# Turning the last gated block inside a down product: a change of order in the expert stage of a decoder step

## The chip, the cores and the metric

The kernel runs on one core of a Trainium2 chip. The metric is the device time of one execution in microseconds; three runs give a median. The profile is of one further execution, with its own time.

The engines have these names in the profile: PE is TensorE (PEld its weight loads), DVE is VectorE, ACT is ScalarE, POOL is GpSimd, SP is SyncE, which only issues transfers here.

## The reference, cut to what matters

One inference step of a two-layer decoder for 256 prompt tokens and 8 sample tokens, width 1024. The part that the change touches is the last one, a top-2-of-8 mixture of SwiGLU experts, each 1024 -> 3584 -> 1024:

```python
def swiglu(h, w1, w3, w2):
    return (jax.nn.silu(h @ w1) * (h @ w3)) @ w2

def moe_swiglu(h, w_router, b_router, w1, w3, w2):
    ...
    for e in range(N_EXPERTS):
        y = swiglu(h, w1[e], w3[e], w2[e]).astype(jnp.float32)
        out = out + dense_gate[..., e:e + 1] * y
```

All inputs are float32, and all eight experts' weights (3 x 1024 x 3584 each) are read once.

## The kernel before

**What came earlier.** Layer 0, the shared keys and values, attention and routing fill the first 775 us or so. Routing scatters the tokens' rows into a table of 128 slots for each expert, and the expert stage takes one expert after the other from it. For experts 0 to 6 the stage is a hardware loop; expert 7 is written out once more behind it.

**A product in three passes.** Every float32 operand is split into a high part (`_hi`, a rounded copy) and a low part (`_lo`, the remainder). A product is hi x hi + hi x lo + lo x hi, three matmuls of 128 x 128 by 128 x 512 each, made by the helper `three` (lines 477 to 479, so most matmuls carry one of these line numbers).

**Slabs.** An expert's weights come in 42 slabs of 1 MB (128 partitions x 2048 float32). The list `eslabs` gives their order. The hidden width is cut into seven blocks `j` of 512. For each block there are two slabs of w1, two of w3, and then the two slabs of w2 for the block before:

```python
for j in range(FCH):
    eslabs += [(1, j, 0), (1, j, 1), (3, j, 0), (3, j, 1)] + ([(2, j - 1, 0), (2, j - 1, 1)] if j else [])
eslabs += [(2, FCH - 1, 0), (2, FCH - 1, 1)]
```

So an expert's last slabs are w3 of block 6, w2 of block 5, w2 of block 6.

**The path of one slab.** SP issues its transfer into one of seven ring slots (`ring`, line 450) as soon as the slab seven places earlier has been split. ACT writes its high part (`w_hi`, `high`, line 1219) into one of three pair buffers: it waits until PE has used the slab three places earlier (`pair_used`) and until the transfer has landed. DVE writes the low part (`w_lo`, `low`, line 1715) when ACT is done with the high one. PE then does the slab's 12 matmuls.

**One expert on PE.** For each block `j`: the w1 product into bank 3 and the w3 product into bank 4 (`product`, 24 matmuls each on the rows `xe_hi`, `xe_lo`); between the two, the gated block of `j - 1` is turned by four PE transposes into bank 5 (`turn`, line 910); after them, `down(j - 1)`, 24 matmuls of the turned block with the two w2 slabs, into banks 6 and 7. Behind the last block the loop has no next w1 product, so three things follow each other on PE: `turn(6)`, then `turn_rows` (line 884: eight transposes of the next expert's rows into banks 0 and 1), then `down(6)`.

**What ACT and DVE do beside the slabs.** Each runs its instructions strictly in the order in which they are written, in a loop over `eslabs` that handles slab `k + 3` at place `k`:
- ACT: `silu` of bank 3 (line 1242) at (1, j, 1); `turned_high`, the high part of bank 5 into `upT_hi` (line 1233), for block `j - 1` right behind it; for block 6 at (2, 5, 1), after that place's `high`; then `gathered_high`, the high part of the next expert's rows (line 1224).
- DVE: the gating product, bank 4 times `silu`, into `up` (line 1741; its tile is named `phase` in the profile) at (3, j, 1), after that place's `low`; `turned_low`, the remainder of bank 5 into `upT_lo` (line 1730), for block `j - 1` at (1, j, 1) and for block 6 at (2, 5, 1), in each case after that place's `low`; then `gathered_low` (line 1720).

PE's `turn` waits for the gating product (`up_ready`) and for the previous remainder (`upT_ready`), and `down(j)` waits for `upT_ready` of block `j`. `turned_high` waits for `up_turned` from PE. The first product of the next expert waits for `xe_ready` from `gathered_low`. POOL stores an expert's output rows and fetches the rows of the next one but one when `turn_rows` has taken the last (512 KB each).

Of the kernel before, what the change touches and what calls it, by code (L numbers as in the profile page):

```python
# [5 lines left out]
F32 = mybir.dt.float32  # L6
F32R = mybir.dt.float32r
I32 = mybir.dt.int32
ALU = mybir.AluOpType
ACT = mybir.ActivationFunctionType  # L10
X = mybir.AxisListType.X

P = 128
# [16 lines left out]
FCH = FE // 512  # L30
# [5 lines left out]
SLOTS = 128  # L36
# [58 lines left out]
def yoco_step(nc, w, o):  # L95
# [24 lines left out]
    with ExitStack() as ctx:  # L120
# [12 lines left out]
        def over(name, other, skip, shape, dt):  # L133

            return nc.alloc_sbuf_tensor_at(name, shape, dt, offset=placed[other] + 4 * skip)
# [5 lines left out]
        bank = [wide[i // 2][:, 512 * (i % 2):512 * (i % 2 + 1)] for i in range(8)]  # L141
# [23 lines left out]
        tT = sb("tT", [P, KC, NT])  # L165
# [98 lines left out]
        gsel = mflat[0:1 + NB, D:D + P]  # L264
        grow = at(10240, D)[0:1 + NB, :]

        upT_hi = over("upT_hi", "tT", 0, [P, 4, P], F32R)
        upT_lo = over("upT_lo", "tT", 512, [P, 4, P], F32R)
        up_s = at(10240, 512)
        up = at(10752, 512)  # L270
        lg = at(11264, 3, NE)
# [23 lines left out]
        pair_used = sem("pair_used")  # L295
# [4 lines left out]
        xe_hi_ready, xe_ready, upT_hi_ready, upT_ready = (sem(n) for n in ("xe_hi_ready", "xe_ready", "upT_hi_ready", "upT_ready"))  # L300
# [75 lines left out]
        def used_by(e, c, m, j, half=1):  # L376

            return e * PER_E + (NSPLIT + c * NE * PER_E + eslabs.index((m, j, half)) + 1)
# [92 lines left out]
        def _(pe):  # L471
# [3 lines left out]
            def three(out, a, b, start, stop):  # L475

                pe.matmul(out, a[0], b[0], start=start, stop=False, skip_group_check=True)  # L477
                pe.matmul(out, a[0], b[1], start=False, stop=False, skip_group_check=True)  # L478
                return pe.matmul(out, a[1], b[0], start=False, stop=stop, skip_group_check=True)  # L479
# [208 lines left out]
            for c in range(LIN):  # L688
                for m in range(2):
                    i = 2 * c + m  # L690
# [160 lines left out]
            for c in range(3):  # L851
                for k in range(c + 1):
                    n = rows[k]
# [34 lines left out]
            def expert(e, c, last):  # L888

                def weights(m, j, half, rows):  # L890
                    k = eslabs.index((m, j, half))
                    pe.wait_ge(lo_done, e * PER_E + (NSPLIT + c * NE * PER_E + k + 1))
                    return [t[:, (NSPLIT + k) % PAIRS, :].rearrange("p (k n) -> p k n", k=rows) for t in (w_hi, w_lo)]

                def count(per, k):
                    return e * per + (c * NE * per + k)

                def product(m, j, bk):
                    for half in range(2):
                        hi, lo = weights(m, j, half, 4)  # L900
                        for i in range(4):
                            k = 4 * half + i
                            mm = three(bank[bk][0:SLOTS, :], (xe_hi[:, k, :], xe_lo[:, k, :]), (hi[:, i, :], lo[:, i, :]), k == 0, k == KC - 1)
                        mm.then_inc(pair_used, 1)

                def turn(j):
                    pe.wait_ge(up_ready, count(FCH, j + 2))
                    pe.wait_ge(upT_ready, count(FCH, j + 1))
                    for i in range(4):
                        mm = pe.transpose(bank[5][:, SLOTS * i:SLOTS * (i + 1)], up[0:SLOTS, P * i:P * (i + 1)], ident[0:SLOTS, 0:SLOTS])  # L910
                    mm.then_inc(up_turned, 1)

                def down(j):
                    pe.wait_ge(upT_ready, count(FCH, j + 2))
                    if j == 0:
                        pe.wait_ge(y0_copied, count(1, 1))
                        pe.wait_ge(y1_copied, count(1, 1))
                    for half in range(2):
                        hi, lo = weights(2, j, half, 2)
                        for i in range(2):  # L920
                            for q in range(2):
                                cols = slice(512 * q, 512 * (q + 1))
                                mm = three(bank[6 + q][0:SLOTS, :], (upT_hi[:, 2 * half + i, :], upT_lo[:, 2 * half + i, :]),
                                           (hi[:, i, cols], lo[:, i, cols]), j == 0 and half == 0 and i == 0, j == FCH - 1 and half == 1 and i == 1)
                        mm.then_inc(pair_used, 1)

                pe.wait_ge(xe_ready, count(1, 1))
                for j in range(FCH):
                    pe.wait_ge(silu_done, count(FCH, j + 1))
                    product(1, j, 3)  # L930
                    if j >= 1:
                        turn(j - 1)
                    pe.wait_ge(up_ready, count(FCH, j + 1))
                    product(3, j, 4)
                    if j >= 1:
                        down(j - 1)
                turn(FCH - 1)
                if not last:
                    turn_rows(e, c, 1)
                down(FCH - 1)  # L940
# [14 lines left out]
        def _(act):  # L955
# [271 lines left out]
            def expert(e, c, last):  # L1227
                def count(per, k):
                    return e * per + (c * NE * per + k)

                def turned_high(j):
                    act.wait_ge(up_turned, count(FCH, j + 1))
                    act.activation(upT_hi[:, :, :], bank[5][:, :].rearrange("p (k n) -> p k n", k=4), ACT.Copy).then_inc(upT_hi_ready, 1)

                for k, (m, j, half) in enumerate(eslabs):

                    if k + PAIRS < PER_E or not last:
                        high(e, c, k + PAIRS)
                    if (m, half) == (1, 1):
                        act.wait_ge(pair_used, used_by(e, c, 1, j))  # L1240
                        act.wait_ge(up_ready, count(FCH, j + 1))
                        act.activation(up_s[0:SLOTS, :], bank[3][0:SLOTS, :], ACT.Silu).then_inc(silu_done, 1)
                        if j >= 1:
                            turned_high(j - 1)
                    if (m, j, half) == (2, FCH - 2, 1):
                        turned_high(FCH - 1)
                        if not last:
                            gathered_high(e, c, 1)
                act.wait_ge(pair_used, used_by(e, c, 2, FCH - 1))
                act.wait_ge(y_free, count(1, 1))  # L1250
                act.activation(ye[0:SLOTS, 0:512], bank[6][0:SLOTS, :], ACT.Copy).then_inc(y0_copied, 1)
# [24 lines left out]
        def _(dve):  # L1276
# [440 lines left out]
            def gathered_low(e, c, ahead):  # L1717
                dve.wait_ge(xe_hi_ready, e + (c * NE + ahead + 1))
                for q in range(2):
                    ins = dve.tensor_tensor(xe_lo[:, 4 * q:4 * q + 4, :], bank[q][:, :].rearrange("p (k n) -> p k n", k=4),  # L1720
                                            xe_hi[:, 4 * q:4 * q + 4, :].bitcast(F32), ALU.subtract)
                ins.then_inc(xe_ready, 1)

            def expert(e, c, last):
                def count(per, k):
                    return e * per + (c * NE * per + k)

                def turned_low(j):
                    dve.wait_ge(upT_hi_ready, count(FCH, j + 1))
                    dve.tensor_tensor(upT_lo[:, :, :], bank[5][:, :].rearrange("p (k n) -> p k n", k=4),  # L1730
                                      upT_hi[:, :, :].bitcast(F32), ALU.subtract).then_inc(upT_ready, 1)

                for k, (m, j, half) in enumerate(eslabs):
                    if k + PAIRS < PER_E or not last:
                        low(e, c, k + PAIRS)
                    if (m, half) == (1, 1) and j >= 1:
                        turned_low(j - 1)
                    if (m, half) == (3, 1):
                        dve.wait_ge(pair_used, used_by(e, c, 3, j))
                        dve.wait_ge(silu_done, count(FCH, j + 2))  # L1740
                        dve.tensor_tensor(up[0:SLOTS, :], bank[4][0:SLOTS, :], up_s[0:SLOTS, :], ALU.mult).then_inc(up_ready, 1)
                    if (m, j, half) == (2, FCH - 2, 1):
                        turned_low(FCH - 1)
                        if not last:
                            gathered_low(e, c, 1)
                dve.wait_ge(pair_used, used_by(e, c, 2, FCH - 1))
                dve.wait_ge(y_free, count(1, 1))
                dve.tensor_copy(ye[0:SLOTS, 512:1024], bank[7][0:SLOTS, :]).then_inc(y1_copied, 1)
# [195 lines left out]
```

## Time and profile before

| | |
|---|---|
| time of the three runs | 1827.14, 1830.06, 1832.4 us; median 1830.06 us |
| the profiled execution | 1819.31 us, of which its span (first to last instruction) 1817.4 us |
| PE busy | 1627.1 us, 90% of the span |
| DVE busy | 1251.6 us, 69% |
| ACT busy | 983.4 us, 54% |
| transfers | 513.45 MB, 283 GB/s over the span |
| transfers of expert slabs | 336 of 1024 KB |
| mean granted PE clock | 0.927 of full speed |

How to read it: the span has stages with different limits, so shares of the whole say little about one stage. What matters here is the stage of the experts, which runs from about 778 us to 1783 us; the rows below are from that stage. Busy PE time includes matmuls that run at the lower of the two clock levels, so a busy PE is not always a fast one.

### The profile page before, as it was taken

What the parts mean: (1) busy time and instruction counts of PE and PEld (TensorE: products, weight loads), DVE (VectorE), ACT (ScalarE), POOL (GpSimd) and SP (SyncE); (2) the same over time, 40 slices, a digit from 0 to 9 for tenths busy, and PEclk for the clock granted to TensorE, in tenths of its full rate; (3) what the DMA queues carried; (4) which work ended last, traced back from release to release, by engine and by line L of the source; (5) the groups of instructions that cost most, each with busy time, mean ns of one, the idle gap of its engine ahead of it and who ended that gap; (6) DMA issues with size and microseconds to landing.
All of it is one profiled execution on the core that took longest, in us unless ns stands there. A gap on an engine that the chain in (4) does not pass through costs nothing.

```text
span 1817.4 us, 22939 instructions
## 1 busy us (share of the span) xinstructions
PE 1627.1 (90%) x8712; PEld 1323.3 (73%) x8712; DVE 1251.6 (69%) x1092; ACT 983.4 (54%) x881; POOL 135.0 (7%) x130
## 2 busy tenths in 40 slices
PE   6869999799897669789999999999999999999991
PEld 3459999498784446578788788788787887887881
DVE  2464543668772442478788788788787887887884
ACT  1134432333332332367677677677676776776771
POOL 0000000026431311100000000000000000000001
PEclk9679999899998759789999999999999999999996
DMA  9965545945468025689999899899899998998972
GB/s 322 349 211 186 180 151 180 304 159 199 161 226 305 0 70 210 243 307 368 333 381 381 309 395 375 309 388 378 310 391 353 345 382 306 388 379 310 387 287 85
DMA packets 249295, 513.45 MB, mean 283 GB/s; under 512 B 9977, under 2 KB 69545, under 8 KB 249217
## 3 DMA queue, kind: packets, MB, share of 16 engines
q1 hardware_dynamic: 243691, 492.49, 75.4%
q0 software_dynamic: 4768, 17.37, 2.5%
q10 hardware_dynamic: 766, 2.65, 0.4%
q8 instruction: 45, 0.74, 0.2%
q14 instruction: 25, 0.20, 0.0%
HBM read 498.58 MB, written 14.35 MB: 282 GB/s over the span
## 4 chain that ended last, share of the span: by engine, by line
PE 76%; DVE 12%; ACT 3%; issue 3%; POOL 3%; DMA 2%; SPq 0%; POOLq 0%; DVEq 0%; ACTq 0%
PE wide L477 22%; PE wide L478 21%; PE wide L479 21%; POOL phase L1787 2%; ACT w_hi L1219 2%; DVE phase L1491 2%; PE wide L537 2%; DVE w_lo L1715 2%; PE wide L526 1%; PE wide L910 1%; POOL phase L1793 1%; DVE w_lo L393 1%; DMA ring<-in_cache_v 1%; PE wide L758 1%; DMA ring<-in_ada_mix_w 1%
## 5 line engine op out<-in xcount | busy, mean ns | idle before, releaser
L1715 DVE TENSOR_TENSOR w_lo<-ring,w_hi 128x2048 fp32r<-128x2048 f32 x336 | 768.3, 2290 | 162.1 <-ACT w_hi L1219 161.7
L1219 ACT ACTIVATE w_hi<-ring 128x2048 fp32r<-128x2048 f32 x336 | 643.5, 1920 | 267.8 <-PE wide L479 267.7
L477 PE MATMUL wide<-w_hi,xe_hi 128*128 128x512 f32 x896 | 355.7, 397 | 6.7 <-DVE xe_lo L1720 5.0
L479 PE MATMUL wide<-w_hi,xe_lo 128*128 128x512 f32 x896 | 350.2, 391 | 0.0
L478 PE MATMUL wide<-w_lo,xe_hi 128*128 128x512 f32 x896 | 349.8, 390 | 0.0
L477 PE MATMUL wide<-tHi,w_hi 128*128 128x264 f32 x672 | 198.4, 295 | 28.2 <-DVE mLo L1409 28.2
L478 PE MATMUL wide<-mLo,w_hi 128*128 128x264 f32 x736 | 212.6, 289 | 0.0
L477 PE MATMUL wide<-w_hi,upT_hi 128*128 128x512 f32 x448 | 184.4, 412 | 27.7 <-DVE upT_lo L1730 27.7
L393 DVE TENSOR_TENSOR w_lo<-ring,w_hi 128x2048 fp32r<-128x2048 f32 (+1 forms) x58 | 138.3, 2388 | 99.6 <-ACT w_hi L973 99.1
L477 PEld LDWEIGHTS wide<-w_hi,xe_hi 128*128 128x128 f32 x896 | 168.9, 188 | 45.0 <-DVE w_lo L1715 6.2
L479 PEld LDWEIGHTS wide<-w_hi,xe_lo 128*128 128x128 f32 x896 | 168.7, 188 | 36.1
L478 PEld LDWEIGHTS wide<-w_lo,xe_hi 128*128 128x128 f32 x896 | 169.0, 189 | 33.4
L479 PE MATMUL wide<-tHi,w_lo 128*128 128x264 f32 x672 | 192.9, 287 | 0.0
L478 PE MATMUL wide<-w_lo,upT_hi 128*128 128x512 f32 x448 | 183.4, 409 | 0.0
L479 PE MATMUL wide<-w_hi,upT_lo 128*128 128x512 f32 x448 | 180.5, 403 | 0.0
L477 PEld LDWEIGHTS wide<-tHi,w_hi 128*128 128x128 f32 x672 | 129.4, 193 | 37.9 <-issue 37.7
L478 PEld LDWEIGHTS wide<-mLo,w_hi 128*128 128x128 f32 x736 | 142.5, 194 | 0.3
L973 ACT ACTIVATE w_hi<-ring 128x2048 fp32r<-128x2048 f32 (+1 forms) x58 | 109.1, 1886 | 61.2 <-PE wide L479 61.1
L479 PEld LDWEIGHTS wide<-tHi,w_lo 128*128 128x128 f32 x672 | 129.0, 192 | 0.0
L477 PEld LDWEIGHTS wide<-w_hi,upT_hi 128*128 128x128 f32 x448 | 88.4, 197 | 50.1 <-DVE w_lo L1715 27.5
L479 PEld LDWEIGHTS wide<-w_hi,upT_lo 128*128 128x128 f32 x448 | 88.5, 198 | 20.6
L478 PEld LDWEIGHTS wide<-w_lo,upT_hi 128*128 128x128 f32 x448 | 88.9, 198 | 18.2
(276 smaller groups left out, 1727.8 us busy)
## 6 DMA issues: line engine op xcount, KB each, us to landing
ring<-in_moe_w SPq DMA_DIRECT2D x336, 1024.0 KB, 7.0
ring<-in_ffn_w SPq DMA_DIRECT2D x30, 1024.0 KB, 5.4
ring<-in_ada_mix_w SPq DMA_DIRECT2D x24, 1024.0 KB, 7.8
ring<-in_ada_ffn_w SPq DMA_DIRECT2D x24, 1024.0 KB, 14.2
ring<-in_w_q SPq DMA_DIRECT2D x12, 1024.0 KB, 8.6
ring<-in_cache_k SPq DMA_DIRECT2D x24, 512.0 KB, 4.9
ring<-in_cache_v SPq DMA_DIRECT2D x24, 512.0 KB, 6.7
ring<-in_w_kv SPq DMA_DIRECT2D x8, 1024.0 KB, 6.4
```

Of the source, the lines that this page charges most:

```text
L393: eng.tensor_tensor(w_lo[:, i % PAIRS, 0:size], ring[:, n % RING, 0:size], w_hi[:, i % PAIRS, 0:size].bitcast(F32), ALU.subtract).then_inc ...
L477: pe.matmul(out, a[0], b[0], start=start, stop=False, skip_group_check=True)
L478: pe.matmul(out, a[0], b[1], start=False, stop=False, skip_group_check=True)
L479: return pe.matmul(out, a[1], b[0], start=False, stop=stop, skip_group_check=True)
L526: mm = pe.matmul(out[32 * k:32 * (k + 1), :], c32[:, 4 * half + k, :], slab_view(n)[:, k, :], start=(half == 0), stop=(half == 1))
L537: mm = pe.matmul(bank[7][:, 0:NT], ones, tT[:, k, :], start=(k == 0), stop=(k == KC - 1))
L758: mm = pe.matmul(bank[b1][:, P * g:P * (g + 1)], qT[part, g * KC + p, early], kT[part, p, early], start=False, stop=True, skip_group_check ...
L973: act.activation(w_hi[:, i % PAIRS, 0:size], ring[:, n % RING, 0:size], ACT.Copy).then_inc(hi_done, 1)
L1219: act.activation(w_hi[:, (NSPLIT + k) % PAIRS, :], ring[:, slot, :], ACT.Copy).then_inc(hi_done, 1)
L1491: ins = dve.tensor_tensor(k_prod[t % 2][:, cols], slab_view(n)[:, t % 2, cols], bank[6 + q], ALU.mult)
L1715: dve.tensor_tensor(w_lo[:, i, :], ring[:, slot, :], w_hi[:, i, :].bitcast(F32), ALU.subtract).then_inc(lo_done, 1)
L1787: pool.tensor_tensor(out, rawT[:, r % 4, :], cos, ALU.mult).then_inc(cos_done, 1)
```

## The change

Three edits, all in the expert stage; no arithmetic changes.

1. `upT_hi` and `upT_lo` become two buffers each, used in turn by block parity, so that block 6 can be written while block 5 is still read.
2. `turn(6)` moves on PE from behind `down(5)` to the place between the two halves (slabs) of `down(5)`. On ACT, `turned_high(6)` moves from behind the `high` of place (2, 5, 1) to ahead of the `high` of place (2, 5, 0), that is, some one slab earlier and ahead of the high part of the expert's last slab. On DVE `turned_low(6)` moves in the same way, ahead of the `low` of place (2, 5, 0).
3. On DVE the gating product of every block, at (3, j, 1), is done ahead of that place's `low` and not behind it.

```diff
-        upT_hi = over("upT_hi", "tT", 0, [P, 4, P], F32R)
-        upT_lo = over("upT_lo", "tT", 512, [P, 4, P], F32R)
+        upT_hi = [over(f"upT_hi{i}", "tT", 1024 * i, [P, 4, P], F32R) for i in range(2)]
+        upT_lo = [over(f"upT_lo{i}", "tT", 1024 * i + 512, [P, 4, P], F32R) for i in range(2)]
...
-                def down(j):
+                def down(j, between=None):
...
                         mm.then_inc(pair_used, 1)
+                        if half == 0 and between is not None:
+                            turn(between)
...
                     if j >= 1:
-                        down(j - 1)
-                turn(FCH - 1)
+                        down(j - 1, between=(j if j == FCH - 1 else None))
                 if not last:
                     turn_rows(e, c, 1)
                 down(FCH - 1)
...
# ACT
                 for k, (m, j, half) in enumerate(eslabs):
 
+                    if (m, j, half) == (2, FCH - 2, 0):
+                        turned_high(FCH - 1)
                     if k + PAIRS < PER_E or not last:
                         high(e, c, k + PAIRS)
...
                     if (m, j, half) == (2, FCH - 2, 1):
-                        turned_high(FCH - 1)
                         if not last:
                             gathered_high(e, c, 1)
...
# DVE
                 for k, (m, j, half) in enumerate(eslabs):
+                    if (m, half) == (3, 1):
+                        dve.wait_ge(pair_used, used_by(e, c, 3, j))
+                        dve.wait_ge(silu_done, count(FCH, j + 2))
+                        dve.tensor_tensor(up[0:SLOTS, :], bank[4][0:SLOTS, :], up_s[0:SLOTS, :], ALU.mult).then_inc(up_ready, 1)
+                    if (m, j, half) == (2, FCH - 2, 0):
+                        turned_low(FCH - 1)
                     if k + PAIRS < PER_E or not last:
                         low(e, c, k + PAIRS)
                     if (m, half) == (1, 1) and j >= 1:
                         turned_low(j - 1)
-                    if (m, half) == (3, 1):
-                        dve.wait_ge(pair_used, used_by(e, c, 3, j))
-                        dve.wait_ge(silu_done, count(FCH, j + 2))
-                        dve.tensor_tensor(up[0:SLOTS, :], bank[4][0:SLOTS, :], up_s[0:SLOTS, :], ALU.mult).then_inc(up_ready, 1)
-                    if (m, j, half) == (2, FCH - 2, 1):
-                        turned_low(FCH - 1)
-                        if not last:
-                            gathered_low(e, c, 1)
+                    if (m, j, half) == (2, FCH - 2, 1) and not last:
+                        gathered_low(e, c, 1)
```

In `turned_high`, `turned_low` and `down` the buffer is picked by `j % 2`.

## Rows read from the trace of the kernel before

**Rows 1.** The page: busy us (share) xcount; granted PE clock in 40 slices, tenths.

```profile
PE 1627.1 (90%) x8712; PEld 1323.3 (73%) x8712; DVE 1251.6 (69%) x1092; ACT 983.4 (54%) x881; POOL 135.0 (7%) x130
...
PEclk9679999899998759789999999999999999999996
```

**Rows 2.** Waits in the expert stage, 775 to 1783 us: us in total, times, longest.

```profile
ACT w_hi L1219 <- PE wide L479: 267.7, 305, 7.1
...
PEld wide L477 <- DVE w_lo L1715: 33.7, 21, 3.9
PE wide L477 <- DVE upT_lo L1730: 27.7, 8, 3.7
```

**Rows 3.** Windows: first matmul of each `down(5)` to the next expert's first product.

```profile
core 0: us, PE busy (x) PEld busy (x) DVE busy (x) ACT busy (x) POOL busy (x), PEclk, DMA share, GB/s
887.70:905.57 17.87, 14.18 (x62) 11.45 (x61) 11.60 (x9) 9.13 (x7) 0.00 (x0) 0.90 0.91 338
...
1769.11:1782.64 13.53, 11.72 (x53) 9.25 (x51) 7.42 (x5) 4.44 (x3) 0.00 (x0) 1.00 0.00 1
sum 145.43, PE 117.76 PEld 94.49 DVE 90.17 ACT 68.34 POOL 0.00; mean PE 14.72 PEld 11.81 DVE 11.27 ACT 8.54 POOL 0.00
```

**Rows 4.** Timeline, PE, end of expert 0: start us, us, instruction.

```profile
887.70 0.39 PE L477 MATMUL wide<-w_hi,upT_hi 128*128 128x512 f32 x1
...
893.20 0.60 PE L910 MATMUL wide<-const,phase 128*128 128x128 f32 x4
893.63 1.04 PE L884 MATMUL wide<-const,hT 128*128 128x128 f32 x8
898.36 0.50 PE L477 MATMUL wide<-w_hi,upT_hi 128*128 128x512 f32 x1 [3.69 <-DVE upT_lo L1730]
...
899.22 0.63 PE L477 MATMUL wide<-w_hi,upT_hi 128*128 128x512 f32 x1
...
905.57 0.40 PE L477 MATMUL wide<-w_hi,xe_hi 128*128 128x512 f32 x1
```

**Rows 5.** Timeline, ACT, the same stretch.

```profile
887.90 1.92 ACT L1219 ACTIVATE w_hi<-ring 128x2048 fp32r<-128x2048 f32 x1 [0.72 <-PE wide L479]
890.64 1.92 ACT L1219 ACTIVATE w_hi<-ring 128x2048 fp32r<-128x2048 f32 x1 [0.82 <-PE wide L479]
...
895.21 0.58 ACT L1233 ACTIVATE upT_hi<-wide 128x512 fp32r<-128x512 f32 x1
895.69 1.08 ACT L1224 ACTIVATE xe_hi<-wide 128x512 fp32r<-128x512 f32 x2
```

**Rows 6.** Timeline, DVE, the same stretch.

```profile
887.21 2.29 DVE L1715 TENSOR_TENSOR w_lo<-ring,w_hi 128x2048 fp32r<-128x2048 f32 x1 [0.40 <-ACT w_hi L1219]
889.85 2.29 DVE L1715 TENSOR_TENSOR w_lo<-ring,w_hi 128x2048 fp32r<-128x2048 f32 x1 [0.35 <-ACT w_hi L1219]
892.06 0.68 DVE L1741 TENSOR_TENSOR phase<-wide,phase 128x512 f32<-128x512 f32 x1
...
895.34 2.29 DVE L1715 TENSOR_TENSOR w_lo<-ring,w_hi 128x2048 fp32r<-128x2048 f32 x1 [0.40 <-ACT w_hi L1219]
897.55 0.68 DVE L1730 TENSOR_TENSOR upT_lo<-wide,upT_hi 128x512 fp32r<-128x512 f32 x1
898.15 1.28 DVE L1720 TENSOR_TENSOR xe_lo<-wide,xe_hi 128x512 fp32r<-128x512 f32 x2
```

**Rows 7.** Windows: behind an expert's start, between two starts, over a whole expert.

```profile
907.00:922.00 15.00, 14.75 (x65) 11.78 (x64) 12.30 (x8) 13.62 (x10) 1.08 (x2) 1.00 0.90 310
922.00:1012.00 90.00, 90.00 (x409) 74.20 (x408) 79.87 (x44) 67.08 (x44) 0.00 (x0) 1.00 1.03 386
1000.00:1120.00 120.00, 116.05 (x515) 94.98 (x514) 100.34 (x57) 86.89 (x60) 1.07 (x2) 0.97 0.96 357
```

**Rows 8.** Line 450, slab transfers: issue to landing, 1040 to 1062, then 1110 to 1136.

```profile
DMA to landing us min/median/max: 7.8/9.1/9.6
...
DMA to landing us min/median/max: 5.5/5.8/7.0
```

More of the change, by code:

```diff
@@ L922, in down @@
                                 cols = slice(512 * q, 512 * (q + 1))
-                                mm = three(bank[6 + q][0:SLOTS, :], (upT_hi[:, 2 * half + i, :], upT_lo[:, 2 * half + i, :]),
+                                mm = three(bank[6 + q][0:SLOTS, :], (upT_hi[j % 2][:, 2 * half + i, :], upT_lo[j % 2][:, 2 * half + i, :]),
                                            (hi[:, i, cols], lo[:, i, cols]), j == 0 and half == 0 and i == 0, j == FCH - 1 and half == 1 and i == 1)
                         mm.then_inc(pair_used, 1)
+                        if half == 0 and between is not None:
+                            turn(between)
                 pe.wait_ge(xe_ready, count(1, 1))
@@ L1232, in turned_high @@
                     act.wait_ge(up_turned, count(FCH, j + 1))
-                    act.activation(upT_hi[:, :, :], bank[5][:, :].rearrange("p (k n) -> p k n", k=4), ACT.Copy).then_inc(upT_hi_ready, 1)
+                    act.activation(upT_hi[j % 2][:, :, :], bank[5][:, :].rearrange("p (k n) -> p k n", k=4), ACT.Copy).then_inc(upT_hi_ready, 1)
                 for k, (m, j, half) in enumerate(eslabs):
+                    if (m, j, half) == (2, FCH - 2, 0):
+                        turned_high(FCH - 1)
                     if k + PAIRS < PER_E or not last:
@@ L1729, in turned_low @@
                     dve.wait_ge(upT_hi_ready, count(FCH, j + 1))
-                    dve.tensor_tensor(upT_lo[:, :, :], bank[5][:, :].rearrange("p (k n) -> p k n", k=4),
-                                      upT_hi[:, :, :].bitcast(F32), ALU.subtract).then_inc(upT_ready, 1)
+                    dve.tensor_tensor(upT_lo[j % 2][:, :, :], bank[5][:, :].rearrange("p (k n) -> p k n", k=4),
+                                      upT_hi[j % 2][:, :, :].bitcast(F32), ALU.subtract).then_inc(upT_ready, 1)
                 for k, (m, j, half) in enumerate(eslabs):
+                    if (m, half) == (3, 1):
[4 more added lines that the diff above has]
+                        turned_low(FCH - 1)
                     if k + PAIRS < PER_E or not last:
```

## The prediction, made before the changed kernel was run

> **What bounds the kernel now.** I read the page first: PE is busy 1627.1 of 1817.4 us, DVE 1251.6, ACT 983.4, and the granted clock is 9 tenths or more nearly all through the second half [rows 1]. The experts fill that half, so PE sets their time and what counts is where PE stands still. Next I read the waits of the expert stage alone. Most rows there are harmless: ACT waits 267.7 us for PE in 305 pieces, which only says that ACT is ahead of its buffers [rows 2]. The row to see is PE waiting for `upT_lo`: 27.7 us in 8 pieces, one for each expert, none over 3.7 us [rows 2]. The 33.7 us of PEld waiting for `w_lo` lie in the same gaps, since its longest piece, 3.9 us, is a weight load in that gap. No row of that view has ACT waiting for a slab's transfer.
>
> Then I cut out the eight stretches from the first matmul of `down(5)` to the next expert's first product (for the last expert, to the end of `down(6)`) and asked for busy time and clock in each. All eight are 145.43 us long with 117.76 us of PE busy; without the last, 131.90 us and 106.04 us [rows 3].
>
> The timelines of one stretch tell why. `down(5)` runs from 887.70 to 893.20, the four transposes to 893.63, then eight more for the next rows, and PE starts `down(6)` only at 898.36 [rows 4]. ACT has first to write the next slab's high part, then 895.21 the block's [rows 5]; DVE first the next slab's remainder (895.34), and only at 897.55 the block's [rows 6]. So two slab passes, 1.92 and 2.29 us, stand ahead of a 0.6 us one on each engine. Behind the gap the matmuls take 0.63 us and not 0.39 [rows 4]: the granted clock has fallen to the lower level (1.2 GHz) after the idle stretch, and the mean of the stretch is 0.90 [rows 3].
>
> **What a stretch costs without the wait.** `down(5)`, 24 matmuls, takes 893.20 - 887.70 = 5.50 us; four transposes take 0.43, so eight take 0.86 [rows 4]. `down(6)` at the full clock is another 5.50. Sum 12.29 us. Seven such: 86.03 us. Now they take 131.90, so 45.87 us can go: 131.90 - 106.04 = 25.86 us of idle PE and 106.04 - 86.03 = 20.01 us of matmuls at the low clock. The last expert has no rows to turn: 11.43 for its 13.53 us, 2.10 to gain [rows 3].
>
> **Does the new order reach 12.29?** I put the durations into the new order for expert 0.
> - *Gating ahead.* DVE's remainder of 887.21 lets its next instruction start 2.21 us later (as 889.85 to 892.06), at 889.42. The product of block 6 then takes 0.68: `up` is ready at 890.10 [rows 6]. PE ends the first half of `down(5)` at 887.70 + 2.75 = 890.45. Spare 0.35 us: `turn(6)` doesn't wait. The remainder behind it starts at 890.10 where it was 889.85, and ends at 892.31.
> - *Turn between the halves.* PE: 890.45 to 890.88, second half to 893.63, rows to 894.49. ACT sees PE 0.20 us after PE moves on (887.90 against 887.70 [rows 4, 5]): `turned_high(6)` at 891.08, and the high part behind it at 891.57 in place of 890.64, because an ACT pass of this size frees the engine after 0.48 us (895.21 to 895.69 [rows 5]). It ends at 893.49.
> - *`turned_low(6)`* follows the remainder at 892.31 and is done at 892.99; PE wants it at 894.49. Spare 1.5 us.
> - *What queues behind.* The remainder of the expert's last slab waits for that high part: 893.52 to 895.81, and PE wants it after the first half of `down(6)`, 897.24. Spare 1.4. Then the next expert's first slab: high part from 893.83, remainder from 895.78, which frees DVE at 897.99, and `xe_lo`, 1.28 us, to 899.27 [rows 6]; ACT's `xe_hi` is over by 896.8. PE wants `xe_lo` at 899.99. Spare 0.72.
> - *Transfers.* The moved waits make the last slab's remainder, and with it SP's issue of the slab seven places on, about 1 us late against PE. The slowest landing is 9.6 us after issue [rows 8], and an issued slab is wanted some 5.5 slabs of 2.75 us later, 15.1 us. So this lateness costs nothing; without that cover it would be 1 us in each of seven loops, 7 us. POOL's fetch of rows hangs on `turn_rows`, which comes no later.
> - *The second buffer* adds no instruction. *Gating ahead* in blocks 0 to 5 is hidden: DVE would otherwise idle until ACT's 1.92 us high part, which waits for the same slab of PE. The bound of what it gains or costs there is the delay of 0.25 us above in six blocks of eight experts, 12 us if all of it reached PE; I take 0, as the next spare is over 1 us.
>
> Sum: 45.87 + 2.10 = 48.0 us. Against the profiled execution's own time, 1819.31 - 48.0 = 1771.3. The median of the runs is 1830.06, 10.75 us above it; I take the saving off that: **1782 us**.
>
> **Can the transfers follow?** A steadier PE wants the same bytes sooner. Over a whole expert the transfers' share is 0.96 at 357 GB/s; between two starts, with PE never idle, it is 1.03 at 386 GB/s for 90 us on end [rows 7]. And in such a stretch the landings get quicker, from 9.1 us median to 5.8 [rows 8]: transfers gain on PE there. If all seven loops (887.70 to 1769.11, 881.4 us [rows 3]) ran at share 1.03, the transfers would want 881.4 x 0.96/1.03 = 821.5 us; I ask for 835.5. Spare 14 us over the seven, 2 us each.
>
> The Trainium skill's page HBM Reference, section Specifications (TRN2), gives an effective bandwidth of about 358 GB/s for each core. It also says there that a core streaming alone measures well above this share, about 425. By the first figure nothing would change, as 357 is what the stage has now; by the second the sum stands. The trace holds with the second: 386 for 90 us.
>
> **Rivals.**
> 1. *The wait moves.* Two spares are small: 0.35 us for `up` ahead of the turn, and 0.72 for `xe_lo` ahead of the next product. If semaphores or the walk are off by 2 us in all, PE waits 2 us in each of seven loops, 14 us: 1796. A wait that short need not bring the low clock back: the last expert's stretch has 1.81 us idle and a mean clock of 1.00 [rows 3]. For: the spares are sums of many rows. Against: every term is a measured one, and the loops are alike.
> 2. *The clock's part stays.* Only idle goes (25.86 + 2.10): 1802. For: the stage has never run without the gaps. Against: 1.00 over 90 us of unbroken matmuls [rows 7].
> 3. *Memory is the bound already.* The gap lets the transfers run ahead, and without it ACT meets slabs that haven't landed. If the stage keeps its 357 GB/s, it keeps its time: 1830. Against: 386, and quicker landings. This is how the lower figure of the Trainium skill's HBM Reference, section Specifications (TRN2), would act here; the rows speak against it.
> 4. *Slower: the gap is the transfers' rest.* At an expert's start the row fetch and the row store, 512 KB each, run among the slabs, and there the rate for a full share is 310/0.90 = 344 GB/s against 386/1.03 = 375 [rows 7]. Now the rate is made up after a pause of the slab issues. If without the pause the whole loop falls to that mixed rate, 881.4 x 357/344 = 914.7 us: 33 us more, 1863. It decides when the sustained rate falls under 357. For: the two rates. Against: that stretch isn't at a full share, and the mixed traffic is 1 MB in 43.
>
> **How the numbers follow.** Forecast 0.76; rival 1 0.10; rival 2 0.04; rival 3 0.06; rival 4 0.04. About 0.3% (5.5 us) is what a measurement of this kernel can tell from no change. Faster: 0.76 + 0.10 + 0.04 = 0.90; same 0.06; slower 0.04. The range reaches up over rival 1 to just short of rival 2, 1800. Below, the unmeasured runs may lose more at the low clock than the profiled one: if all 24 matmuls of each `down(6)` ran at it, 24 x (0.63 - 0.39) = 5.8 us in seven loops, 40 and not 20.0; with two thirds of that difference 13 more could go: 1769. It leaves out rivals 2 to 4, 0.14, and small tails.
>
> **What the new profile would show.** Right: the row of PE waiting for `upT_lo` gone or under 3 us in all; the seven stretches 12.3 to 12.8 us each with a clock of 1.00; mean share of transfers in a loop near 1.01; the four transposes standing alone between two halves of 12 matmuls. Wrong at a step: PE waiting for `up` or `xe_lo` at the loop's end (rival 1); matmuls of 0.63 us without a gap ahead of them (rival 2); ACT waiting for transfers, and landings of 12 us and more (rivals 3 and 4). What would spoil the prediction most is a memory rate in the timed runs that is lower than in the profiled one, which their 10.75 us might be.

## The result, and the profile after

| | before | after |
|---|---|---|
| median of the runs, us | 1828.7 (1827.14 to 1832.4, 4 runs) | 1780.24 (1772.25 to 1785.46, 4 runs) |
| profiled execution, us (span) | 1819.31 (1817.4) | 1784.68 (1782.8) |
| expert stage in the profile, us | 1004.44 | 956.90 |

The kernel before has one run more here than the three known when the forecast was made. The ratio of the runs, after to before, is 0.9752, with a 95% interval of 0.9718 to 0.9786; the two medians alone give 0.9735. The forecast was 1782 in a range of 1769 to 1800. The expert stage is taken here, and in all that follows, from the first matmul of expert 0's first product to the end of expert 7's last down product; before it ran from 778.20 to 1782.64 us, after from 791.47 to 1748.37.

First the windows of the kernel after: the stretches that answer to [rows 3], of which the five left out are 12.32 or 12.33 us long, then one whole loop, and the whole stage. Columns as in [rows 3].

```profile
901.20:913.55 12.35, 12.35 (x61) 10.24 (x60) 11.58 (x9) 9.13 (x7) 0.00 (x0) 1.00 1.02 354
1020.73:1033.05 12.32, 12.32 (x62) 10.23 (x60) 11.58 (x9) 9.12 (x7) 0.00 (x0) 1.00 0.99 347
...
1736.92:1748.37 11.45, 11.45 (x53) 9.22 (x51) 7.42 (x5) 4.32 (x3) 0.00 (x0) 1.00 0.01 1
...
1020.73:1140.21 119.48, 119.22 (x541) 98.03 (x540) 105.65 (x60) 91.28 (x61) 1.07 (x2) 1.00 1.01 373
...
791.47:1748.37 956.90, 955.37 (x4312) 785.65 (x4312) 836.69 (x466) 720.36 (x480) 6.99 (x13) 1.00 0.99 367
```

The same loop and the whole stage of the kernel before:

```profile
1012.71:1138.70 125.99, 122.04 (x541) 99.89 (x540) 105.67 (x60) 91.26 (x61) 1.07 (x2) 0.97 0.96 358
778.20:1782.64 1004.44, 974.98 (x4312) 798.27 (x4312) 836.86 (x466) 720.63 (x480) 6.99 (x13) 0.98 0.95 349
```

In each stretch PE is busy from end to end and the clock is 1.00. The seven sum to 86.29 us where they were 131.90, and the last expert's is 11.45 where it was 13.53. That is 45.61 + 2.08 = 47.7 us; the stage as a whole has lost 47.54. A loop moves the same bytes in 119.48 us and not 125.99, at share 1.01 and 373 GB/s in place of 0.96 and 358.

The waits of the same stage, the answer to [rows 2] (us in total, times, longest):

```profile
ACT w_hi L1220 <- PE wide L479: 212.5, 297, 0.9
...
ACT upT_hi L1234 <- PE wide L910: 10.1, 8, 1.3
...
PEld wide L477 <- DVE w_lo L1717: 5.8, 14, 0.7
...
PE wide L477 <- DVE w_lo L1717: 1.5, 6, 0.3
```

The row of PE waiting for `upT_lo` is gone. A new row stands in its place one engine on: ACT waits 1.3 us per expert for the turn. It costs nothing. The 1.5 us in 6 pieces are an old wait, 0.3 us behind the start of experts 1 to 6, and the only one that PE has left inside the loops.

The timelines at the end of expert 0 show the new order on PE, ACT and DVE; they answer to [rows 4 to 6].

```profile
901.20 0.39 PE L477 MATMUL wide<-w_hi,upT_hi 128*128 128x512 f32 x1
...
903.95 0.60 PE L910 MATMUL wide<-const,phase 128*128 128x128 f32 x4
904.31 0.48 PE L477 MATMUL wide<-w_hi,upT_hi 128*128 128x512 f32 x1
...
907.17 1.04 PE L884 MATMUL wide<-const,hT 128*128 128x128 f32 x8
907.96 0.48 PE L477 MATMUL wide<-w_hi,upT_hi 128*128 128x512 f32 x1
...
913.55 0.40 PE L477 MATMUL wide<-w_hi,xe_hi 128*128 128x512 f32 x1
```

```profile
904.59 0.60 ACT L1234 ACTIVATE upT_hi<-wide 128x512 fp32r<-128x512 f32 x1 [1.27 <-PE wide L910]
905.09 1.91 ACT L1220 ACTIVATE w_hi<-ring 128x2048 fp32r<-128x2048 f32 x1
```

```profile
902.92 0.68 DVE L1739 TENSOR_TENSOR phase<-wide,phase 128x512 f32<-128x512 f32 x1
903.52 2.28 DVE L1717 TENSOR_TENSOR w_lo<-ring,w_hi 128x2048 fp32r<-128x2048 f32 x1
905.72 0.69 DVE L1732 TENSOR_TENSOR upT_lo<-wide,upT_hi 128x512 fp32r<-128x512 f32 x1
907.02 4.59 DVE L1717 TENSOR_TENSOR w_lo<-ring,w_hi 128x2048 fp32r<-128x2048 f32 x2 [0.62 <-ACT w_hi L1220]
911.53 1.28 DVE L1722 TENSOR_TENSOR xe_lo<-wide,xe_hi 128x512 fp32r<-128x512 f32 x2
```

Read the three against each other. The gating product ends at 903.60, and the four transposes start at 903.95, right behind 12 matmuls: 0.35 us of spare. The block's remainder ends at 906.41, and PE wants it at 907.96. `xe_lo` ends at 912.81, and PE wants it at 913.55: 0.74 us.

One number doesn't fit at first sight: the profiled execution lost 34.6 us and the stage 47.5. The difference was given back ahead of the stage, in code without an edit: expert 0 starts 13.27 us later than in the profile of before. The last two runs below deal with that.

### The profile page after: what moved, and what is told of

Same layout as the page of the kernel before. It is cut to its first block, busy times and chain, and to the rows that moved or that the text cites. A ratio compares the mean times of both kernels' runs of the same rounds, so it can differ in the third digit from the quotient of the medians.

```text
span 1782.8 us, 22939 instructions
## 1 busy us (share of the span) xinstructions
PE 1614.7 (91%) x8712; PEld 1317.8 (74%) x8712; DVE 1251.4 (70%) x1092; ACT 982.8 (55%) x881; POOL 134.9 (8%) x130
## 4 chain that ended last, share of the span: by engine, by line
PE 78%; DVE 11%; DMA 3%; POOL 3%; issue 2%; ACT 2%; SPq 0%; POOLq 0%; DVEq 0%; ACTq 0%
PE wide L477 22%; PE wide L478 22%; PE wide L479 22%; POOL phase L1789 2%; DVE phase L1493 2%; PE wide L526 1%; PE wide L910 1%; POOL phase L1795 1%; PE wide L758 1%; PE wide L537 1%; DVE w_lo L1717 1%; DMA ring<-in_ada_ffn_w 1%; DVE w_lo L393 1%; DMA ring<-in_cache_v 1%; PE wide L512 1%
## 5 line engine op out<-in xcount | busy, mean ns | idle before, releaser
L477 PE MATMUL wide<-w_hi,upT_hi 128*128 128x512 f32 x448 | 177.0, 395 | 0.0
L478 PE MATMUL wide<-w_lo,upT_hi 128*128 128x512 f32 x448 | 176.0, 393 | 0.0
L479 PE MATMUL wide<-w_hi,upT_lo 128*128 128x512 f32 x448 | 174.4, 389 | 0.0
L479 PEld LDWEIGHTS wide<-w_hi,upT_lo 128*128 128x128 f32 x448 | 84.1, 188 | 19.0
L477 PEld LDWEIGHTS wide<-w_hi,upT_hi 128*128 128x128 f32 x448 | 84.1, 188 | 18.4
L478 PEld LDWEIGHTS wide<-w_lo,upT_hi 128*128 128x128 f32 x448 | 84.3, 188 | 16.5
```

## The experiments

The stage's length is the measure in most of them, since it is free of what happens ahead of it.

**Gating ahead, alone.** The kernel before with one move on DVE:

```diff
                 for k, (m, j, half) in enumerate(eslabs):
+                    if (m, half) == (3, 1):
+                        ... (the gating product)
                     if k + PAIRS < PER_E or not last:
                         low(e, c, k + PAIRS)
...
-                    if (m, half) == (3, 1):
-                        ... (the gating product)
```

> The kernel before with the gating product alone moved ahead of the slab's remainder; the turn and its two halves stay where they were, one buffer. The expert stage (first matmul of expert 0's first product to the end of expert 7's last down product) took 1004.4 us before and 956.9 us with the whole change. Theory (the wait is made by the slab passes that stand ahead of the block's two halves on ACT and DVE): the product isn't what PE waits for at the loop's end, so the stage stays at 1004 us, within 1 us. Rival (the later remainders of block 0 to 5 matter, the bound of 0.25 us in six blocks of eight experts): 1016 us. Rival (the gating product is what holds the turn up): 985 us or less.

The stage took 1004.32 us, in the window of the stage:

```profile
780.14:1784.46 1004.32, 974.94 (x4312) 798.73 (x4312) 836.76 (x466) 720.37 (x480) 7.00 (x13) 0.98 0.95 349
```

So the move alone neither gains nor costs; both rivals fall.

**The change without gating ahead.** The gating product goes back behind `low`; the rest of the change stays.

```diff
                 for k, (m, j, half) in enumerate(eslabs):
-                    if (m, half) == (3, 1):
-                        ... (the gating product)
                     if (m, j, half) == (2, FCH - 2, 0):
                         turned_low(FCH - 1)
                     if k + PAIRS < PER_E or not last:
                         low(e, c, k + PAIRS)
                     if (m, half) == (1, 1) and j >= 1:
                         turned_low(j - 1)
+                    if (m, half) == (3, 1):
+                        ... (the gating product)
```

> The changed kernel with the gating product back behind the slab's remainder. Theory: the turn between the halves of the down product then waits for the product. The remainder stands ahead of it for 2.3 to 2.5 us, the wait is too short to bring the low clock back, eight such waits: stage 956.9 + 8 x 2.4 = 976 us, all of it PE waiting for the gating product ahead of the four transposes. Rival (a wait of this length does bring the low clock, some 2.9 us more per expert): 999 us. Rival (moving the product ahead was of no use): 957 us.

Measured 985.66 us, between the theory's 976 and the rival's 999. The stretches of experts 0, 1, 2 and 7 and the stage:

```profile
900.64:916.97 16.33, 14.14 (x61) 11.36 (x60) 11.78 (x9) 9.12 (x7) 0.00 (x0) 0.90 0.80 273
1024.12:1038.87 14.75, 12.56 (x61) 10.16 (x60) 11.76 (x9) 9.13 (x7) 0.00 (x0) 1.00 0.85 297
1146.05:1162.37 16.32, 14.13 (x62) 11.29 (x60) 11.77 (x9) 9.12 (x7) 0.00 (x0) 0.90 0.91 305
1761.14:1776.54 15.40, 13.21 (x53) 10.41 (x51) 7.61 (x5) 4.32 (x3) 0.00 (x0) 0.89 0.00 1
790.88:1776.54 985.66, 966.60 (x4312) 791.68 (x4312) 838.37 (x466) 720.52 (x480) 7.01 (x13) 0.99 0.97 356
```

PE's wait for the gating product, in the run's waits:

```profile
PE wide L910 <- DVE phase L1745: 17.5, 8, 2.2
```

The wait is what was expected: 14.75 - 12.33 = 2.4 us where the clock holds (2.2 by the rows, which draw the last matmul over part of the gap). But it holds in two of eight experts only, 1 and 4. In the other six the stretch is 1.6 us longer still at a mean clock of 0.89 or 0.90. 8 x 2.4 + 6 x 1.6 = 28.8 us, which is 985.66 - 956.90. So gating ahead is worth nothing alone and 28.8 us as a part of the change: it clears the way for the turn.

**PE's part alone.** The change, but ACT and DVE keep the old places for the block's two parts:

```diff
 # ACT, and in the same way DVE with turned_low
-                    if (m, j, half) == (2, FCH - 2, 0):
-                        turned_high(FCH - 1)
...
                     if (m, j, half) == (2, FCH - 2, 1):
+                        turned_high(FCH - 1)
                         if not last:
                             gathered_high(e, c, 1)
```

> The changed kernel (two buffers, gating ahead, PE turns block 6 between the halves), but ACT and DVE write the block's two parts at the old place, behind the slab pass of the place after. Theory: PE's own order is worth nothing, because the two parts come as late as before: PE idles some 4.2 us ahead of the last down product and the clock falls again, stage 1004 to 1008 us. Rival (the early turn on PE is what saves the time): 957 to 965 us.

Measured 1005.65 us. The stretches of experts 0 and 1:

```profile
899.58:917.91 18.33, 14.20 (x61) 11.39 (x60) 11.60 (x9) 9.12 (x7) 0.00 (x0) 0.91 0.83 297
1025.04:1044.18 19.14, 15.01 (x62) 12.03 (x60) 11.60 (x9) 9.12 (x7) 0.00 (x0) 0.82 0.78 284
```

```profile
PE wide L477 <- DVE upT_lo L1731: 30.7, 8, 4.1
```

PE idles 4.1 us in each, for the block's remainder as before, and the clock falls as before. Turning earlier is worth nothing while two slab passes stand ahead of the block's parts.

**The order on ACT and DVE alone.** The kernel before, one buffer, PE as it was; only these two moves:

```diff
 # ACT
+                    if (m, j, half) == (2, FCH - 2, 1):
+                        turned_high(FCH - 1)
                     if k + PAIRS < PER_E or not last:
                         high(e, c, k + PAIRS)
...
                     if (m, j, half) == (2, FCH - 2, 1):
-                        turned_high(FCH - 1)
                         if not last:
                             gathered_high(e, c, 1)
 # DVE: the same with turned_low, low and gathered_low
```

> The kernel before with one edit alone: at the place where ACT and DVE write the parts of block 6, each does so ahead of the slab pass and not behind it. One buffer, gating behind, PE's order as before. Theory: PE turns at the same time as before, the high part follows 0.2 us later, the remainder of the block ends some 1.1 us after the rows are turned, so PE idles 1.1 us per loop at the full clock, and the last expert gains nothing: stage 1004.4 - 45.9 + 7 x 1.1 = 966 us, that is four fifths of the change's gain, and about 1790 us for the whole. Rival (two buffers and the turn inside the down product are needed): 1004 us, 1828 us for the whole.

Measured 968.72 us for the stage and 1793.16 for the whole (median of 4, beside 1820.65 for 7 runs of the kernel before; ratio 0.9819, interval 0.9751 to 0.9887). Expert 0's stretch and the last:

```profile
896.37:909.95 13.58, 12.57 (x61) 10.31 (x60) 11.58 (x9) 9.13 (x7) 0.00 (x0) 1.00 1.00 351
1740.92:1756.03 15.11, 13.30 (x53) 10.39 (x51) 7.42 (x5) 4.44 (x3) 0.00 (x0) 0.89 0.01 2
```

All seven stretches are 13.58 or 13.59 us at clock 1.00: PE idles about 1.25 us, and that brought the low clock in none of them. The last stretch is 1.6 us longer than before, with the low clock behind the same 1.8 us of idle time that left it at 1.00 before [rows 3]. In the last expert of the runs with gating ahead alone, with PE's part alone and with the filled gap such a wait left it at 1.00 too. So two moved lines and no buffer give 35.7 of the 47.5 us. The other 11.8 us come with the turn between the halves and the second buffer together; no run has one of these two without the other.

**The gap, filled.** The kernel before with work for PE in the gap:

```diff
                 if not last:
                     turn_rows(e, c, 1)
+                    for _ in range(32):
+                        pe.transpose(bank[2][:, 0:P], ident, ident)
                 down(FCH - 1)
```

> The kernel before, with 32 more transposes of the unit matrix on PE behind the turning of the next rows, into a bank that nothing reads, in experts 0 to 6. They end before the turned block is ready, so PE starts the last down product as late as before. Theory (20.0 of the 48.0 us are matmuls at 1.2 GHz behind an idle stretch): with PE kept busy the clock stays at 2.4 GHz and the stage loses the clock's part alone: 1004.4 - 20 = 984 us, granted clock 1.00 in the stretches. Rival (the clock falls for another reason, or transposes don't hold it): 1004 us.

Measured 986.53 us. Expert 1's stretch, before and in this run, and in this run the fill, the first matmul behind it and DVE's write of the block's remainder:

```profile
1012.71:1031.52 18.81, 15.12 (x61) 12.15 (x60) 11.66 (x9) 9.13 (x7) 0.00 (x0) 0.82 0.78 286
...
1012.45:1028.73 16.28, 16.07 (x94) 13.80 (x92) 11.58 (x9) 9.13 (x7) 0.00 (x0) 1.00 0.91 331
...
1019.25 3.66 PE L941 MATMUL wide<-const 128*128 128x128 f32 x32
1023.12 0.50 PE L477 MATMUL wide<-w_hi,upT_hi 128*128 128x512 f32 x1 [0.21 <-DVE upT_lo L1732]
...
1022.31 0.69 DVE L1732 TENSOR_TENSOR upT_lo<-wide,upT_hi 128x512 fp32r<-128x512 f32 x1
```

The remainder ends 10.55 us into the stretch, where it was 10.53 in [rows 4, 6], and PE still waits 0.21 us for it behind the fill: the wait is untouched. All seven stretches are 16.27 or 16.28 us, 113.93 in all against 131.90: with the clock held, 18.0 us go. What is left above 86.29 us, 27.6, is the wait. So the two terms are shown each by itself, and they are 27.6 and 18.0, where the forecast had 25.9 and 20.0.

**One ring slot fewer.** The change with `RING = 6` in place of 7.

> The changed kernel with six ring slots in place of seven, so that each slab's transfer is issued one slab, some 2.75 us, later. Theory (transfers have spare: a slab lands at least 4.9 us ahead of ACT's pass on it): the stage stays at 957 us within 1 us, with landings some 2 to 7 us ahead, and ACT never waits for a transfer. Rival (without the gap the transfers are close to being the bound): ACT waits for transfers, PE for remainders, stage 962 us or more.

Measured 955.75 us, 1.15 less than with seven, just outside the 1 us that the theory allowed; 0.85 of it lies ahead of expert 0's `down(5)` (108.88 us against 109.73). The landings, from 920 us to the end of the stage, of this run and then of the changed kernel:

```profile
DMA to landing us min/median/max: 4.9/7.2/9.6
...
DMA to landing us min/median/max: 4.9/7.2/10.1
```

No row of this run's waits in the stage has ACT waiting for a transfer. The time from a slab's landing to the start of ACT's pass on it, taken for each slab but expert 0's first 12, is 2.6 us at the least, and 4.9 with seven slots. So a lead shorter by about a slab costs nothing: at this pace of PE the transfers are not the bound. How much faster PE could go before they were, no run shows.

**Ahead of the stage.** The change with one addition in the prompt's attention, and the change once more beside it on the same chip:

```diff
                 if p + n:
                     pe.wait_ge(a_copied, 2 * p + n)
                 else:
                     pe.wait_ge(sv_summed, 1)
+                for _ in range(24 if n else 4):
+                    pe.transpose(bank[6][:, 3 * P:4 * P], ident, ident)
+                pe.wait_ge(a_norm, 2 * p + n + 1)
```

(The wait for `a_norm` stood ahead of the other.)

> The changed kernel with one addition in code that the change doesn't touch: in the prompt's attention (some 575 to 655 us), ahead of each wait for the normalised weights, PE does 4 or 24 transposes of the unit matrix into columns that nothing reads. The profiled execution of the changed kernel came to its first expert product at 791.5 us, that of the kernel before at 778.2, with no edit in between; the difference opens between 585 and 655 us, where the granted clock is lower. Theory (the times of one kernel spread by where the clock falls there, not by the expert stage): with the clock held, the first expert product comes at 775 us or sooner, the stage stays 956.9 us, the whole is 1765 us or less and its runs lie closer together. Rival (the spread has another cause, or the added transposes stand in the way of the chain): first product at 785 us or later, spread as before.

> The changed kernel once more, unaltered, beside the one above on the same chip. Theory: stage 956.9 us within 0.5 us again, since PE is never idle in it for more than 0.4 us; whatever the whole time does comes from ahead of the first expert product. Rival (the stage itself varies from execution to execution, with the transfers): stage off by 2 us or more.

Windows of the attention and of the stage: the run with the fill, the second profiled execution of the changed kernel, and its first.

```profile
575.00:655.00 80.00, 65.54 (x453) 51.53 (x451) 40.31 (x70) 30.95 (x71) 24.22 (x24) 0.89 0.23 81
778.09:1734.85 956.76, 955.24 (x4312) 785.65 (x4312) 836.42 (x466) 720.46 (x480) 6.99 (x13) 1.00 0.99 367
```

```profile
575.00:655.00 80.00, 51.61 (x260) 36.38 (x262) 37.55 (x64) 28.77 (x64) 24.12 (x24) 0.70 0.20 67
779.35:1735.92 956.57, 954.79 (x4312) 785.20 (x4312) 836.41 (x466) 720.42 (x480) 7.00 (x13) 1.00 0.99 367
```

```profile
575.00:668.00 93.00, 62.55 (x264) 43.94 (x264) 39.80 (x68) 29.44 (x65) 24.16 (x24) 0.56 0.17 57
```

And, in the same order, the attention from its first to its last score matmul, and from there to the first expert product:

```profile
557.29:655.28 97.99, 81.59 (x546) 59.63 (x546) 46.44 (x80) 35.59 (x81) 28.20 (x28) 0.91 0.38 135
655.28:778.09 122.81, 93.73 (x589) 69.24 (x590) 45.32 (x101) 36.96 (x74) 16.27 (x21) 0.79 0.52 190
...
557.12:661.89 104.77, 72.24 (x373) 47.67 (x372) 46.34 (x80) 35.59 (x81) 28.12 (x28) 0.74 0.36 126
661.89:779.35 117.46, 87.75 (x539) 63.26 (x538) 45.30 (x101) 36.97 (x74) 16.25 (x21) 0.76 0.54 197
...
557.09:672.95 115.86, 82.70 (x373) 55.01 (x372) 46.38 (x80) 35.54 (x81) 28.14 (x28) 0.62 0.32 114
672.95:791.47 118.52, 87.93 (x538) 64.09 (x538) 45.33 (x101) 36.70 (x74) 16.24 (x21) 0.74 0.54 196
```

The stage is 956.76 and 956.57 us, as the first time. The changed kernel's second profiled execution took 1772.85 us and comes to the experts at 779.35; its first was 12 us later there, and 11 of these lie in the attention, 115.86 us at a clock of 0.62 against 104.77 at 0.74. In the five runs of this series the shortest has the highest mean clock (1772.85 us, 0.937) and the two longest the two lowest (1783.42 and 1784.86 us, 0.927 and 0.929). With the fill the clock is 0.89 in the window from 575 us, the median is 1767.3 us (1765.83 to 1772.33, 5 runs) against 1779.04 (1772.85 to 1784.86, 5 runs) without, and the intervals of the ratios to before, 0.9660 to 0.9723 and 0.9734 to 0.9804, don't overlap. The profiled one was the slowest of the five, and came to the experts at 778.09, not by 775 as forecast; the whole is 2 us over the 1765 forecast. Its attention is 6.8 us shorter than the unfilled one at 0.74, but the code behind it, without an edit, is 5.4 us longer, and no run shows why. So the theory is right in direction and spread, and too hopeful in size: that the attention gets shorter with the clock is shown, that all of the 11.7 us between the medians comes of it is not. This is the fastest version of the study.

## Why the prediction was right, step by step

*What bounds the kernel.* Right: PE sets the experts' time. With its gaps gone, PE is busy 955.37 of 956.90 us.

*12.29 us for a stretch.* Measured 12.32 to 12.35, and 11.45 for the last expert where 11.43 was forecast. The walk of durations through the new order held to a few hundredths: spare of 0.35 us ahead of the turn, as forecast, and 0.74 ahead of the next product, for 0.72.

*48.0 us in all.* The stage lost 47.54. The eight stretches gave 47.7, and the way from expert 0's first product to its `down(5)`, 0.2 us longer than before, took a little back.

*25.86 us of idle time and 20.01 of slow clock.* The sum was right and the split mis-sized: 27.6 and 18.0 by the filled gap. The split had been taken from PE's busy time, whose matmuls are drawn past the start of the next (0.39 us long, 0.23 us apart), so part of the gap had been counted as busy: 3.69 us of idle time by the rows [rows 4], 16.28 - 12.33 = 3.95 by the filled gap. The lower end of the range has the same misreading. It took 0.63 - 0.39 us as what a matmul costs more at the low clock, which is a difference of drawn lengths; the matmul behind the one at 899.22 [rows 4] starts 0.43 us later, so it is 0.20, and the lower end would be some 1773 and not 1769. The result lies inside either way.

```profile
899.65 0.63 PE L478 MATMUL wide<-w_lo,upT_hi 128*128 128x512 f32 x1
```

*Gating ahead at nothing in blocks 0 to 5.* Right: 0.1 us by itself. That it carries 28.8 us at the loop's end was not costed separately; the walk had it as the 0.35 us of spare.

*The second buffer, and ACT's pass held up by the turn.* Right: ACT waits 1.3 us in each expert and its slab pass comes later. DVE waits 0.62 us for that pass (0.40 before), and PE not at all.

*Transfers can follow.* Right: a share near 1.01 in a loop was forecast, 1.01 is measured, and a ring slot was to spare. The Trainium skill's HBM Reference, section Specifications (TRN2), has about 358 GB/s for a core and about 425 for a core that streams alone; 373 GB/s over a whole loop is on the side of the second.

*The rivals.* A wait that moves (rival 1): none came. But the claim under it, that a wait of 2 us need not bring the low clock, held only in part: 2.4 us brought it in six of eight experts. Had the gating product been late by a slab pass, the price would have been 28.8 us and not 19. Rivals 2 to 4 didn't happen.

*The saving taken off the median.* Right for the median: 1828.7 - 1780.24 = 48.5 us. That the median came within 2 us of 1782 is in part luck: the four runs lie between 1772.25 and 1785.46, and in the later series the two medians, 1825.01 and 1779.04, are 46.0 us apart. Nor can whole runs tell 5.5 us from no change, as the forecast took it: nine runs of the kernel before lay between 1816.77 and 1831.33 there. What held closely is the stage, 47.54 for 48.0. For the two profiled executions the saving is 34.6 us, in the main because the attention ran at another clock in the second: by the same windows as above, 104.98 us at 0.74 before and 115.86 at 0.62 after. The forecast had the 10.75 us between the median and the profiled execution as a possible lower memory rate. The later runs speak for the clock ahead of the experts: the stage is the same to 0.4 us in three executions while the start of it moves by 13. What sets the clock's course there in one execution and not in another stays open.

The Trainium skill's page TensorE: Matmul & The Clock Gate, section HAM oscillation — how this bites in real kernels, says that idle gaps between groups of matmuls put the engine back to its lower level, so that each group starts slow. The filled gap agrees: the same wait with PE kept busy has a clock of 1.00 and costs 18.0 us less.

## What to carry to other kernels

When an engine waits for a short operation, look at what stands ahead of it in the queue of the engine that does it: here two slab passes of 1.92 and 2.29 us stood ahead of two of 0.6, and moving two lines gave 75% of the gain without a buffer. The parts of such a change don't add up one by one (0.1 us for gating alone, 28.8 as a part), so walk all of them through the new order with durations from the trace and note the spare at each wait. And cost a gap on PE with the matmuls behind it: 18.0 of the 45.6 us in the loops were not idle time but a low clock.

## What the runs showed of the hardware that was not expected

The same idle time on PE doesn't always bring the low clock. Counted as the length of a stretch above the unbroken one where the clock held (for the longest, with the gap filled): 1.25 us brought it in none of seven stretches; 2.0 or 2.1 us, in the last expert, not in the kernel before nor in three runs that wait as it does, but in the run with the order alone; 2.4 us in six of eight; and some 3.9 us in all seven. What decides it between equal gaps stays open.

Where PE works in short bursts, as in the attention from 575 us, the mean clock differs between executions of the same code: from the first to the last score matmul it was 0.62 and 0.74 in the two of the changed kernel, and the attention took 115.86 us at the lower, 104.77 at the higher. Transposes of a constant, put where PE waits, raised it to 0.91 and shortened it to 97.99; the median of the whole fell by 11.7 us.
